# Sliding-window attention beside its output projection: the pipeline of a block made one block longer, with transposes and logits in another order

## What is computed

```python
q = rms_norm((rms_norm(x, g_norm) @ w_q) per head, g_q)     # 16 heads of 64, 4 K/V heads
logits = einsum("bntkgd,bnskd->bnkgts", q, k_band) * HEAD_DIM ** -0.5
logits = where(mask, logits - slopes * dist, -inf)          # 8 blocks of 128 tokens, keys: own and previous block
m = maximum(max(logits), sink)
p = exp(logits - m)
p = p / (sum(p) + exp(sink - m))
o = einsum("bnkgts,bnskd->bntkgd", p, v_band)
x = x + o.reshape(b, s, 1024) @ w_o
```

## Time and profile before

| what | value |
| --- | --- |
| time, median of 3 runs | 2137.26 us (2134.13 to 2141.6) |
| time of the profiled execution | 2137.56 us, its span 2135.4 us |
| mean granted TensorE clock | 0.983 |
| busy share of the span | PE 95%, PE weight loads 80%, DVE 66%, ACT 42%, POOL 20% |
| attention stage | about 1178 to 1430 us of the span |
| chain that ended last, over the whole span | PE 81%, DVE 13%, issue 3%, ACT 2%, POOL 1% |

### The profile page before, as it was taken

The page is one execution under the profiler, slowest core; times in us unless marked ns, Lnnn a source line. Parts: engine busy times, 40 slices in busy tenths (PEclk is TensorE's granted clock), DMA queues, the critical chain, the costliest instruction groups (busy, mean ns, idle before and its releaser), DMA issues.

```text
span 2135.4 us, 29061 instructions
## 1 busy us (share of the span) xinstructions
PE 2020.5 (95%) x9972; PEld 1704.1 (80%) x9972; DVE 1402.1 (66%) x2050; ACT 906.7 (42%) x1533; POOL 427.4 (20%) x300
## 2 busy tenths in 40 slices
PE   4999899999999999999899688879899999999999
PEld 4988788788888888888799577767788888888887
DVE  4345658988788864444643677769888887863433
ACT  4233334644444443343211677754544444443332
POOL 3000001233323300001010344422333333300000
PEclk9999899999999999999899899999999999999999
DMA  3111143122122244342011000012122122254433
GB/s 142 41 50 41 48 148 109 60 79 82 75 98 79 88 187 188 147 148 108 20 40 65 16 11 10 20 59 79 60 80 97 64 93 79 94 213 163 175 141 120
DMA packets 44720, 192.96 MB, mean 90 GB/s; under 512 B 4336, under 2 KB 4464, under 8 KB 32368
## 3 DMA queue, kind: packets, MB, share of 16 engines
q1 hardware_dynamic: 44656, 192.12, 24.6%
HBM read 156.45 MB, written 35.65 MB: 90 GB/s over the span
## 4 chain that ended last, share of the span: by engine, by line
PE 81%; DVE 13%; issue 3%; ACT 2%; POOL 1%; DVEq 0%; ACTq 0%; POOLq 0%
PE banks L1965 27%; PE banks L1966 26%; PE banks L1967 26%; DVE lg L1879 2%; DVE t_lo L1470 1%; DVE pT_lo L1829 1%; DVE t_sum L1662 1%; DVE t_sum L1460 1%; DVE o_lo L1837 1%; ACT o_hi L1153 1%; DVE fw_lo L1452 1%; DVE small L1886 0%; POOL nrm L572 0%; DVE xT L1552 0%; DVE fw_lo L1513 0%
## 5 line engine op out<-in xcount | busy, mean ns | idle before, releaser
L1965 PE MATMUL banks<-t_hi,fw_hi 128*128 128x512 f32 x1760 | 688.8, 391 | 12.8 <-issue 11.0
L1967 PE MATMUL banks<-t_hi,fw_lo 128*128 128x512 f32 x1760 | 686.1, 390 | 0.0
L1966 PE MATMUL banks<-t_lo,fw_hi 128*128 128x512 f32 x1728 | 673.8, 390 | 0.0
L1965 PEld LDWEIGHTS banks<-t_hi,fw_hi 128*128 128x128 f32 x1760 | 331.3, 188 | 87.2 <-issue 14.9
L1967 PEld LDWEIGHTS banks<-t_hi,fw_lo 128*128 128x128 f32 x1760 | 331.3, 188 | 69.2
L1966 PEld LDWEIGHTS banks<-t_lo,fw_hi 128*128 128x128 f32 x1728 | 325.4, 188 | 67.5 <-issue 0.5
L1608 DVE TENSOR_TENSOR fw_lo<-raw,fw_hi 128x512 fp32r<-128x512 f32 x120 | 84.2, 703 | 188.7 <-ACT fw_hi L977 188.7
L591 POOL TENSOR_TENSOR nrm<-raw 128x512 f32<-128x512 f32 x40 | 53.6, 1341 | 740.6 <-DVE fw_lo L1513 439.5
L930 ACT ACTIVATE xT<-xT,par 128x1024 f32<-128x1024 f32 x88 | 109.4, 1245 | 161.6 <-DVE xT L1539 118.2
L977 ACT ACTIVATE fw_hi<-raw 128x512 fp32r<-128x512 f32 x120 | 75.6, 631 | 211.2 <-PE banks L1967 211.2
L1552 DVE SCALAR_TENSOR_TENSOR xT<-xT,par 128x1023 f32<-128x1023 f32 x88 | 151.4, 1720 | 0.0
(11 more groups left out here) (184 smaller groups left out, 3685.5 us busy)
## 6 DMA issues: line engine op xcount, KB each, us to landing
raw<-in_w_f_in SPq DMA_DIRECT2D x44, 1024.0 KB, 4.8
raw<-in_w_f_out SPq DMA_DIRECT2D x44, 1024.0 KB, 4.8
c_scratch<-xT SPq DMA_DIRECT2D x44, 512.0 KB, 2.6
c_raw<-c_scratch SPq DMA_DIRECT2D x44, 512.0 KB, 5.6
w_raw<-in_w_ao SPq DMA_DIRECT2D x16, 512.0 KB, 3.4
x_scratch<-xT SPq DMA_DIRECT2D x4, 2048.0 KB, 7.5
xT<-x_scratch SPq DMA_DIRECT2D x4, 2048.0 KB, 12.8
xT<-in_x_t SPq DMA_DIRECT2D x16, 256.0 KB, 6.5
```

Source lines behind the costliest of these rows:

```text
L1965: nc.tensor.matmul(out, w_h, m_h, start=start, stop=False, **kw)
L1966: nc.tensor.matmul(out, w_h, m_l, start=False, stop=False, **kw)
L1967: return nc.tensor.matmul(out, w_l, m_h, start=False, stop=stop, **kw)
```

## The change

Everything stands one block further apart. TensorE's order in block `n` becomes `q_transpose(n+1)`, two outputs, `p_transpose(n-1)`, `logits(n+1)`, `weighted(n-2)`; the transposes, which now stand ahead of `weighted`, wait for `pT_ready` of the block before, since banks 2 and 3 are single. `pT_hi` and `pT_lo` get two buffers. `o_upper` and `o_lower` of a block move one block on, and so do the outputs: group 0 issues two of them (in block 7) instead of four, and two more come behind the last group. On ACT `q_upper(n+2)` moves from in front of the exponentials of block n to behind them, and `v_upper` into blocks 0 and 1. On POOL `v_lower` of both halves moves behind `probabilities(0)` and `(1)`. The two `split`s move from blocks 4 and 6 to 5 and 7. DVE makes one of the two adds ahead of the wait for the exponentials and the other behind the denominators. The instructions of the program are the same in kind and number.

```diff
 def step_outs(n):
-    o = (2 * n + 4) % (2 * KT)
+    o = (2 * n + 2) % (2 * KT)
...
-        pT_hi = sb("pT_hi", [P, 2, QPK * P], F32R)
-        pT_lo = sb("pT_lo", [P, 2, QPK * P], F32R)
+        pT_hi = sb("pT_hi", [P, 2, 2, QPK * P], F32R)
+        pT_lo = sb("pT_lo", [P, 2, 2, QPK * P], F32R)
```

On POOL:

```diff
             def core(j, first):
                 q_lower(j, 0, 1)
-                v_lower(j, 0)
                 q_lower(j, 1, 2)
                 for n in range(NCH):
                     if n + 2 < NCH:
                         q_lower(j, n + 2, 3)
                     probabilities(n)
-                    if n == 1:
-                        v_lower(j, 1)
+                    if n < 2:
+                        v_lower(j, n)
...
-                        if n == 4:
+                        if n == 5:
                             split(0)
-                        if n == 6:
+                        if n == 7:
                             split(1)
```

On ACT:

```diff
                 for n in range(NCH):
-                    old = n >= 2 or (n == 1 and not first)
-                    if old:
-                        p_upper((n - 2) % NCH)
+                    if n >= 2:
+                        p_upper(n - 2)
+                    if n >= 3:
+                        o_upper(n - 3)
+                    elif n == 1 and not first:
+                        o_upper(7, 1)
                     if n + 1 < NCH:
                         q_copy(2)
-                    if n + 2 < NCH:
-                        q_upper(j, n + 2)
                     act.wait_ge(negm_done, blk.now(1))
...
-                    if old:
-                        o_upper((n - 2) % NCH)
-                    if n == 1:
-                        v_upper(j, 1)
+                    if n + 2 < NCH:
+                        q_upper(j, n + 2)
+                    if n < 2:
+                        v_upper(j, n)
```

On DVE:

```diff
                     nc.vector.tensor_tensor(sink_arg, negm, sinks, ALU.add).then_inc(negm_done, 1)
-                    if old:
-                        p_lower((n - 2) % NCH)
-                    if not first or n >= 6:
-                        add_step_outs(n, (0, 1) if n else (1,))
+                    if n >= 2:
+                        p_lower(n - 2)
+                    if n >= 3:
+                        o_lower(n - 3)
+                    elif n == 1 and not first:
+                        o_lower(7, 1)
+                    outs_now = (n and not first) or n == 7
+                    if outs_now:
+                        add_step_outs(n, (0,))
                     dve.wait_ge(exp_done, blk.now(1))
...
-                    if old:
-                        o_lower((n - 2) % NCH)
+                    if outs_now:
+                        add_step_outs(n, (1,))
```

On TensorE:

```diff
             def p_transpose(m, prior=True):
                 pe.wait_ge(p_done, blk.now())
+                if prior:
+                    pe.wait_ge(pT_ready, blk.now(-1))
...
                 if not first:
-                    weighted(6, True)
+                    step_out(0, 1)
                     p_transpose(7)
+                    weighted(6)
                 pe.wait_ge(kT_ready, grp.now())
                 logits(0, 1)
                 for n in range(NCH):
                     if n + 1 < NCH:
                         q_transpose(2)
-                    if (n and not first) or n >= 6:
+                    if n == 0 and not first:
+                        weighted(7, 1)
+                    if (n and not first) or n == 7:
                         step_out(n, 0)
-                    if not first or n >= 6:
                         step_out(n, 1)
+                    if n:
+                        p_transpose(n - 1, not first or n > 1)
                     if n + 1 < NCH:
                         logits(n + 1, 2)
-                    if n >= 2 or (n == 1 and not first):
-                        weighted((n - 2) % NCH, not first or n > 2)
-                    if n:
-                        p_transpose(n - 1)
+                    if n >= 2:
+                        weighted(n - 2, 0, not first or n > 2)
                     blk.add()
```

More of the change, by code:

```diff
@@ L1167, in core @@
                     p_upper(6)
+                    o_upper(5)
                 act.wait_ge(kT_full, grp.add())
@@ L1215, in _ @@
             p_upper(6)
+            o_upper(5)
+            p_upper(7, 1)
+            blk.add()
             o_upper(6)
             blk.add()
-            p_upper(7)
             o_upper(7)
@@ L1823, in _, with p_lower, o_lower @@
             sums, sink_exp = small[:, 7, 0:4], small[:, 7, 4:8]
-            def p_lower(m):
+            def p_lower(m, off=0):
                 st = slice(1 if m == 0 else 0, 2)
-                dve.wait_ge(pT_hi_done, blk.now(-1))
-                nc.vector.tensor_tensor(pT_lo[:, st, :], banks[:, 2 + st.start:4, :],
-                                        pT_hi[:, st, :].bitcast(F32), ALU.subtract).then_inc(pT_ready, 1)
-            def o_lower(m):
-                dve.wait_ge(o_hi_done, blk.now(-1))
+                dve.wait_ge(pT_hi_done, blk.now(off - 1))
+                nc.vector.tensor_tensor(pT_lo[:, m % 2, st, :], banks[:, 2 + st.start:4, :],
+                                        pT_hi[:, m % 2, st, :].bitcast(F32), ALU.subtract).then_inc(pT_ready, 1)
+            def o_lower(m, off=0):
+                dve.wait_ge(o_hi_done, blk.now(off - 2))
                 o_ps = banks[:, 7, :].rearrange("p (m e t) -> p m e t", m=2, e=2)
@@ L1846, in core @@
             def core(j, first):
-                if not first:
-                    p_lower(6)
                 nc.vector.tensor_copy(sinks, par[:, bass.ds(j * QPK + COL_SINK, QPK)])
@@ L1853, in core @@
                 last.then_inc(bias_done, 1)
+                if not first:
+                    p_lower(6)
+                    o_lower(5)
+                    add_step_outs(0, (0,))
                 if first:
@@ L1863, in core @@
                 if not first:
-                    add_step_outs(0, (0,))
-                if not first:
-                    o_lower(6)
+                    p_lower(7, 1)
+                    add_step_outs(0, (1,))
+                    o_lower(6, 1)
                 dve.wait_ge(bias_done, grp.now())
                 for n in range(NCH):
-                    old = n >= 2 or (n == 1 and not first)
                     b0 = 1 if n == 0 else 0
@@ L1905, in _ @@
             p_lower(6)
+            o_lower(5)
             add_step_outs(0)
+            p_lower(7, 1)
+            blk.add()
             o_lower(6)
+            add_step_outs(1)
             blk.add()
-            p_lower(7)
-            add_step_outs(1)
             o_lower(7)
+            add_step_outs(2)
             for k in range(2, KT):
@@ L2298, in logits, with weighted @@
                 mm.then_inc(lg_full, 1)
-            def weighted(m, wait_o):
-                pe.wait_ge(pT_ready, blk.now(-1))
+            def weighted(m, off=0, wait_o=True):
+                pe.wait_ge(pT_ready, blk.now(off - 1))
                 if wait_o:
-                    pe.wait_ge(o_ready, blk.now(-2))
+                    pe.wait_ge(o_ready, blk.now(off - 2))
                 if m in (0, 4):
@@ L2374, in _ @@
             step_out(0, 0)
-            weighted(6, True)
+            step_out(0, 1)
             p_transpose(7)
-            step_out(0, 1)
+            weighted(6)
             blk.add()
@@ L2380, in _ @@
             step_out(1, 1)
-            weighted(7, True)
+            weighted(7)
             blk.add()
+            step_out(2, 0)
+            step_out(2, 1)
             pe.wait_ge(o_ready, blk.now(-2))
```

36 lines of the change are left out of this document (17 added, 19 removed).

## The result

| what | before | after |
| --- | --- | --- |
| median | 2136.7 us (4 runs, 2134.13 to 2141.6) | 2122.27 us (4 runs, 2121.64 to 2126.6) |
| profiled execution, its span | 2137.56, 2135.4 | 2121.64, 2119.5 |
| mean granted TensorE clock | 0.983 | 0.985 |

The changed kernel takes 0.9934 of the time (95% interval 0.9912 to 0.9956). That is faster by 0.66%, 14 us.

What follows compares the result with a forecast made beforehand. It took the loop through p_lower, weighted, o_lower and the next masking to bound steady blocks; group 0 -2.2, three groups +1.2 and the end -5.2 summed to -6.2, from 2137.3 to 2131.0 us, range 2118 to 2140.

Steps and rivals of the forecast that it cites:

- Steady block 6.42: Undisturbed attention blocks: TensorE has no wait left, 6.42 us a block, 0.4 less, 1.6 a group.
- The splits hold negm in block 6: Block 6: split(0) on GpSimd makes DVE's negm wait, so TensorE's transposes start 1.0 us late.
- The start of a group: From block 7 into the next group: TensorE waits 2.1, 1.2, 2.2, 1.2, 0.7 us, and 0.3 at q_transpose(4).
- The loop branch: GpSimd's loop branch ahead of q_lower(0) at a group's start: bounded by 0 to 0.6 us, 0.3 taken.
- Three groups +1.2: Three distances between block-7 starts: 60.6 us each against 60.2, +1.2 us together; groups under 59 would show it wrong.
- Group 0, -2.2: First group, without outputs: block 7 comes 2.2 us sooner, between -3.4 (full clock) and +3.2 (half clock throughout).
- the clock rival: Half clock for 7 of 25 us in each group start loses 10.4 us, group 0 5.4 more: 2147, chance 0.12.
- The end, -5.2: From block 7 of group 3 to the square adds: 18.1 us instead of 23.3, 5.2 less.
- Faster (2117): Rival: GpSimd's instructions don't meet negm, so a group takes about 57.6 us: 2117, chance 0.17.
- a clock under 0.9 in a start: Sign of a wrong forecast: granted TensorE clock under 0.9 in the starts of groups.
- the hold of `bias_j`: Rival: GpSimd's split(1) also holds DVE's four bias_j instructions, p_lower(6) at 11 instead of 8.1; 0.4 a group, 2132, chance 0.29 unsplit.
- The end's gain: Rival: a weight transfer or the saved x sets when the FFN starts, 5.2 us back: 2136, chance 0.13.

Runs made afterwards that it cites:

- e4: Changed kernel with p_transpose(n-1) moved back to the end of TensorE's block, the longer distance kept: 2143.34 us, ratio to before 1.0025.
- e6: Kernel before the change with only TensorE's new order and two buffers of split p, o and outputs not moved: 2195.33 us, ratio to before 1.0268.
- e5: Changed kernel with GpSimd's part of each output-weight split in the loop writing 8 of 1024 columns: 2115.65 us, ratio to before 0.9901.
- e10: Changed kernel with v_lower and splits in GpSimd's gap ahead of q_lower, plus q_upper(2) and (3) ahead of the exponentials of blocks 0 and 1: 2107.59 us, ratio 0.9851.
- e11: The e10 kernel with DVE's o_lower(6) ahead of the add before it at a group's start: 2109.54 us, ratio to before 0.9858.
- e8: Changed kernel with splits, v_upper, v_lower and q_upper all back at their old places: 2118.89 us, ratio to before 0.9903.
- e2: Changed kernel with v_upper and v_lower back at their places before the change: 2124.94 us, ratio to before 0.9941.
- e3: Changed kernel with the splits of weights back in blocks 4 and 6: 2119.85 us, ratio to before 0.9919.
- e7: Changed kernel with the edits of e2 and e3 together: 2121.7 us, ratio to before 0.9922.

## Why the prediction was right, and where it was wrong

The mechanism was right in its main parts. The size was not: the sum was -6.2 us, the stage gave -11.05. Of the 8.7 us by which the forecast was too slow, 4.85 lie in the stage (4.6 in the three groups, 0.5 at the end, less 0.25 in group 0) and 3.9 outside it, where the forecast had no term. That the result still lies in the range owes something to the range's width.

- **Steady block 6.42:** 6.43, no wait. e4 and e6 show that order and distance carry it together.
- **The splits hold negm in block 6:** 2.13 us, and TensorE waits 0.79 to 0.82 us for it, where 1.0 was laid out. e5 shows the cause.
- **The start of a group:** five waits stand where they were laid out, 1.55, 0.93, 2.03, 0.88, 0.39 for 2.1, 1.2, 2.2, 1.2, 0.7; the 0.3 at `q_transpose(4)` does not exist. The loop branch, for which 0.3 was taken, cost nothing: `q_lower(0)` starts at 1347.13, as the split ends.
- **Three groups +1.2: the step that failed.** They gave -3.4. I took all three starts as alike. The start of group 1 follows group 0, whose split(1) is in block 2, so nothing stands ahead of its `q_lower(0)`, there is no wait ahead of `q_transpose(0)`, and group 1 takes 57.65. That is under the 59 that the prediction named as a sign of being wrong. Groups 2 and 3 take 59.88 and 59.69 for 60.6. The listed waits of group 3 are 1.9 us shorter than laid out (6.8 against 8.7), but the 0.8 for first matmuls behind waits was too small: 59.69 less 51.1 of work and 6.8 of waits leaves 1.8. Of the 4.6 us, 3.0 are in group 1 and 1.6 in the other two.
- **Group 0, -2.2:** -1.95, with `logits(4)` 3.7 later (29.90 against 26.18 from the k transposes) where 4 was laid out. This close a hit is partly luck: e10 and e11, whose group 0 is the same, differ by 3.7 us there. The bound of +3.2 for half clock throughout is a slip: 5.4 on top of a term that already holds 1.2 gives +2.0, and the 2147 of the clock rival becomes 2146 in the same way.
- **The end, -5.2:** -5.7. The squares start at 1416.28, 17.6 us behind block 7, where 18.1 was laid out.
- **Outside the stage:** 5 us ahead of attention in the profiled pair, which no term had. They match the 10 us less at half clock there; why the clock fell less often in that execution is open. Over the 14 profiles the two go together: half clock up to 1160 lasts 27 us where attention starts earliest (1168.73) and 44 us in the three where it starts last (1175.66 to 1176.32). The change's own part, 11.05, lies inside the interval of the ratio (9 to 19 us).
- **Rivals.** Faster (2117): the result lies between it and the forecast, but not by its mechanism, since GpSimd did meet `negm`. Slower by the clock: the first 10 us of group 2's start are at full clock, and the stretch behind them is not,

```profile
1285.00:1295.00 10.00, 7.46 (x47) 5.87 (x45) 9.94 (x14) 5.61 (x10) 3.76 (x3) 1.00 0.14 52
1300.00:1310.00 10.00, 9.93 (x49) 8.21 (x49) 7.97 (x25) 6.04 (x19) 5.78 (x5) 0.84 0.00 0
```

  so here the sign of a clock under 0.9 in a start did show. It cost little: TensorE was at half clock for 3.4 us from 1299, the waits of 0.88 and 0.39 are missing in that group, and it takes 59.88 where group 3, at full clock, takes 59.69. DVE is busy 9.94 of 10 us in the first window, of which some 2.65 are the hold of `bias_j`: 3.79 us instead of 1.14. That hold was a rival of its own, a side case in the forecast; it said that no row showed a `tensor_scalar` between SBUF tiles held, but `negm` in the earlier trace rows is one. `p_lower(6)` comes 9.5 us behind block 7, and most of that hid behind the wait ahead of `q_transpose(0)`. The end's gain was not lost. The Trainium skill, "SBUF — State Buffer", section "Who interferes with whom", lets copies and `tensor_scalar` between SBUF tiles into 2-port modes, which exclude GpSimd; the trace agrees, the copy of four numbers (1.50 us, 0.16 before the change) included.

## What to carry to other kernels

Before moving an instruction on GpSimd, look at which small DVE instruction between SBUF tiles runs beside its new place, and whose wait hangs on it. Then put the GpSimd instruction into the gap of that loop by a wait on a semaphore that is already there. Here this took another 15.9 us off the attention stage (267.60 to 251.70; the ratio to the kernel before went from 0.9934 to 0.9857) without removing any work. That is more than the 11.05 of the change itself. A longer pipeline paid here only where every edge of the loop got longer: one buffer (e4) or one in-order engine (e6) that kept its old distance set the old time, or a worse one. And a sum over "three groups" needs each of them looked at, the first above all.

## What the hardware showed that I had not expected

- A DVE copy of 128x4 between SBUF tiles took 1.50 us instead of 0.16, and four `tensor_scalar` of 128x256 took 3.79 us instead of 1.14. Behind a hold GpSimd's next instruction could get in first: in e8 the sum, free at 1308.51, waited for the `q_lower` of 1308.41 as well. GpSimd's own rows kept their length (2.34 to 2.42 us for each full split of the stage) in every kernel: here it is DVE that waits.
- The same code ahead of attention took 1168.7 to 1176.3 us in 14 profiles, 0.36% of the span, at mean granted clocks of the whole execution of 0.976 to 0.985. An effect of 2 to 3.5 us (e2, e3, e7) is not seen in medians of four runs. It shows in the distances between the groups; even the stage's own length carries group 0, which differed by 3.7 us between e10 and e11.
